# Activation halves, the weights' low half and the feed-forward halves at other SBUF addresses

## The reference, cut to what matters

```python
for i in range(DEPTH):                       # DEPTH = 2
    mod = c_act @ ada_w[i] + ada_b[i]        # 2048 x 12288 weights per layer, one row
    sh1, sc1, g1, sh2, sc2, g2 = split(mod, 6)
    h = x * (1.0 + sc1) + sh1
    y = mixer_ab(h, ...) if i % 2 == 0 else mixer_cd(h, ...)   # h @ w_in, heads, @ w_out
    x = layer_norm(ALPHA * x + (1.0 + g1) * y, ...)
    h = x * (1.0 + sc2) + sh2
    y = (silu(h @ w_gate) * (h @ w_up)) @ w_down               # D_FF = 5632
    x = layer_norm(ALPHA * x + (1.0 + g2) * y, ...)
```

## Time and profile before

| | |
|---|---|
| median of 3 runs | 3096.1 us (3093.45 to 3096.98) |
| the profiled execution, its time | 3097.86 us |
| its span, first to last instruction | 3096.1 us |
| mean granted PE clock in the span | 0.907 of 2.4 GHz |
| PE busy | 2681.2 us, 87% |
| DVE busy | 2090.0 us, 68% |
| ACT busy | 1103.0 us, 36% |
| read from memory | 611.73 MB, 198 GB/s over the span |

### The profile page before, as it was taken

One profiled execution on the slowest core, in us unless ns is written; L12 is line 12 of the kernel. 1 busy time (PEld: TensorE's weight loads), 2 busy tenths in 40 slices (PEclk: granted clock), 3 DMA queues, 4 the chain that ended last, 5 costly groups with the idle time before them and its releaser, 6 DMA issues.

```text
span 3096.1 us, 43878 instructions
## 1 busy us (share of the span) xinstructions
PE 2681.2 (87%) x16756; PEld 2429.2 (78%) x16756; DVE 2090.0 (68%) x2403; ACT 1103.0 (36%) x1089; POOL 477.2 (15%) x614
## 2 busy tenths in 40 slices
PE   2398887566679799999999978999888999999997
PEld 1387777455569688988998968999877899889887
DVE  6879998566756677677777758746766754444454
ACT  0234444322213433333333342344334333333333
POOL 1059996111110000000000001100000000000000
PEclk6599999755569899999999989999999999999998
DMA  9752323233337478878788738944547765555551
GB/s 341 249 203 97 107 97 109 68 107 108 108 136 249 140 265 284 278 268 291 268 282 282 264 107 314 323 155 155 204 162 243 273 206 197 184 188 193 191 188 68
DMA packets 287583, 615.63 MB, mean 199 GB/s; under 512 B 22220, under 2 KB 22755, under 8 KB 286947
## 3 DMA queue, kind: packets, MB, share of 16 engines
q1 hardware_dynamic: 252642, 479.64, 45.9%
q0 software_dynamic: 34816, 134.23, 12.2%
HBM read 611.73 MB, written 2.10 MB: 198 GB/s over the span
## 4 chain that ended last, share of the span: by engine, by line
PE 66%; issue 14%; DVE 11%; POOL 4%; ACT 4%; DMA 1%; DVEq 0%; SPq 0%; POOLq 0%; ACTq 0%
PE groups L1518 10%; PE groups L1510 10%; PE groups L1514 10%; PE groups L1512 10%; PE groups L1522 10%; PE groups L1520 10%; DVE w_lo L1161 2%; PE pm L1489 1%; PE pb L1573 1%; ACT w_hi L950 1%; PE pa L1568 1%; DMA ada_units<-in_ada_w_dram 1%; ACT act_hi L1010 1%; POOL dn_mb L614 1%; DVE ada_acc L1352 1%
## 5 line engine op out<-in xcount | busy, mean ns | idle before, releaser
L1161 DVE TENSOR_TENSOR w_lo<-w_raw,w_hi 128x2048 fp32r<-128x2048 f32 x388 | 894.3, 2306 | 715.0 <-ACT w_hi L950 707.2
L950 ACT ACTIVATE w_hi<-w_raw 128x2048 fp32r<-128x2048 f32 x386 | 738.8, 1915 | 1287.9 <-PE groups L1522 681.5
L1518 PE MATMUL groups<-act_hi,w_hi 128*128 128x256 f32 x1984 | 582.6, 294 | 66.9 <-DVE w_lo L1161 33.1
L1510 PE MATMUL groups<-w_hi,act_hi 128*128 128x512 f32 x1408 | 556.0, 395 | 35.3 <-DVE w_lo L1161 20.9
L1520 PE MATMUL groups<-act_lo,w_hi 128*128 128x256 f32 x1984 | 571.9, 288 | 0.0
L1522 PE MATMUL groups<-act_hi,w_lo 128*128 128x256 f32 x1984 | 571.2, 288 | 0.0
L1514 PE MATMUL groups<-w_lo,act_hi 128*128 128x512 f32 x1408 | 552.2, 392 | 0.0
L1512 PE MATMUL groups<-w_hi,act_lo 128*128 128x512 f32 x1408 | 552.2, 392 | 0.0
L1151 DVE SCALAR_TENSOR_TENSOR ada_acc<-ada_units,c_act,ada_acc 128x512 f32<-128x512 f32 x600 | 467.4, 779 | 24.3 <-DMA ada_units<-in_ada_w_dram 7.0
L1518 PEld LDWEIGHTS groups<-act_hi,w_hi 128*128 128x128 f32 x1984 | 392.1, 198 | 81.5 <-DVE w_lo L1161 39.6
L1520 PEld LDWEIGHTS groups<-act_lo,w_hi 128*128 128x128 f32 x1984 | 392.1, 198 | 0.2
(11 more groups left out here) (335 smaller groups left out, 2511.5 us busy)
## 6 DMA issues: line engine op xcount, KB each, us to landing
ada_units<-in_ada_w_dram POOLq DMA_DIRECT2D x128, 1024.0 KB, 6.1
w_raw<-in_ffn_w_gate_dram SPq DMA_DIRECT2D x88, 1024.0 KB, 5.6
w_raw<-in_ffn_w_up_dram SPq DMA_DIRECT2D x88, 1024.0 KB, 5.4
w_raw<-in_ffn_w_down_dram SPq DMA_DIRECT2D x88, 1024.0 KB, 5.2
w_raw<-in_cd_w_in_dram SPq DMA_DIRECT2D x48, 1024.0 KB, 5.6
ada_units<-in_ada_w_dram SPq DMA_DIRECT2D x40, 1024.0 KB, 5.0
w_raw<-in_ab_w_in_dram SPq DMA_DIRECT2D x40, 1024.0 KB, 5.0
ada_first<-in_ada_w_dram SPq DMA_DIRECT2D x24, 1024.0 KB, 9.2
```

The lines of the kernel that those rows point to most:

```text
L950: act.activation(whi[:, j % 2], raw[:, (j + 2) % 4], ACT.Copy).then_inc(hi_done, 1)
L1161: dve.tensor_tensor(wlo[:, half], raw[:, slot], whi[:, half].bitcast(F32), ALU.subtract).then_inc(lo_done, 1)
L1510: pe.matmul(dst, hi[:, k, rows], whi[:, j % 2, kk], start=(k == 0), stop=False, skip_group_check=True)
L1518: pe.matmul(dst, whi[:, j % 2, kk, cols], hi[:, k], start=(q == 0 and kk == 0 and n % 2 == 0), stop=False, skip_group_check=True)
```

## The change

No instruction changes; only where tiles lie. Three small tiles (704 bytes) are declared ahead of `ada_first`, the low half of the weights is declared behind the activation halves instead of ahead of them, and two tiles that nothing uses (320 and 192 bytes) are put on either side of it.

```diff
+        dcw = sb("dn_conv_cols", [P, 4 * 3 * HT])
+        misc = sb("misc_cols", [P, 64])
+        cact = sb("c_act", [P, KT])
         (first6,) = shared([("ada_first", [P, FIRST_SLOTS - 2, UK, GROUP])])
-        wlo = sb("w_lo", [P, 2, UK, GROUP], F32R)
         ahi = sb("act_hi", [P, KT, L], F32R)
         alo = sb("act_lo", [P, KT, L], F32R)
+        sb("w_lo_shift", [P, 80])
+        wlo = sb("w_lo", [P, 2, UK, GROUP], F32R)
+        sb("hid_shift", [P, 48])
         mod = sb("mod", [P, DEPTH * N_ADA])
         adab = sb("ada_b_cols", [P, DEPTH * N_ADA])
         lnc = sb("ln_cols", [P, 4 * DEPTH * KT])
-        dcw = sb("dn_conv_cols", [P, 4 * 3 * HT])
-        misc = sb("misc_cols", [P, 64])
         ident = sb("ident", [P, P])
         ones = sb("ones", [P, P])
-        cact = sb("c_act", [P, KT])
```

## The result

| | before | after |
|---|---|---|
| median of 20 runs each | 3095.7 us (3088.4 to 3101.3) | 3100.9 us (3091.9 to 3110.8) |
| ratio after to before | | 1.0021 [1.0012, 1.0029] |
| the profiled execution, its time and span | 3097.9, 3096.1 us | 3098.7, 3096.9 us |
| mean granted PE clock | 0.907 | 0.911 |

The time lies inside the range, but on the other side of no change than forecast: 0.2% slower, not 0.25% faster. That it lies inside is luck: the range reached above 3096 us for the rival in which `hid`'s own 512 bytes cost time, and they cost none (experiment 2).

A forecast was written before the change was run, and what follows sets the result against it. The prediction took about 60% of the span as a PE matmul stream, bound by the distance between starts. Savings of 4.8 and 3.2 us, together 8.0, gave 3089.9 us (3088 against the median); range 3066 to 3104 us.

The forecast's parts named there:

- The cause of the difference between `act` and `hid`: Narrow matmuls: operands 0 bytes apart on act, 704 on hid, modulo 1,024; this distance makes 120.0 against 113.3 or 118.1 ns.
- the rival that something else was at work: Narrow matmuls on act: address is not the cause, act stays at 120.0 ns, time at 3096 us; chance 0.13.
- `act` in the narrow form: Mixer stages' narrow matmuls on act reach hid's levels: 3,150 matmuls on the path, 8.0 us saved.
- I take middle: In in0u, out0, in1a, out1, narrow matmuls fall from 120.0 to 118.1 ns: 2,406 by 2.0 ns, 4.8 us.
- `hid`. Cost: nothing: Down products on hid: the 512-byte move costs nothing, bounded by 23 us lost and 5 us gained.
- The parity argument: For hid, distances over the two column-block parities only swap, {704, 192} to {192, 704}, so its level stays.
- `hid` loses: Rival: the 512 bytes turn hid's quick stretches slow, costing 23 us, less 8 on act: 3111 us; chance 0.17.
- The small tiles and `ada_first` have few reads: nothing: Moving the small tiles and ada_first has no effect on time.
- I take it that the wide form pays no conflict now and can hide one after: nothing: Wide form, 227.0 ns: its changed operand distance neither gains nor costs; bound of 42 us on a gain.
- The sum: Whole kernel: 8.0 us saved, the profiled execution going from 3097.9 to 3089.9 us.
- The Trainium skill's rule: PE has two independent read ports, so weight loads take no matmul read bandwidth; by it the saving would be 0.

The follow-up runs named there:

- experiment 2: The run hid_only: the kernel before with only the shared region, which holds the hid tile, moved by 512 bytes; 3093.9 us, ratio 0.9997.
- distances_64: Sweep with PE alone, reference computation left out: activation halves 0 to 960 bytes past weight halves, by 64; at distance 0 narrow about 120 ns, wide 226.7 to 228.1.
- hid_only: The kernel before with only the shared region moved by 512 bytes, act and w_lo in place; 3093.9 us, ratio 0.9997 to before.
- ident64: The kernel before with c_act declared ahead of ident and ones, moving only these two by 64 bytes; 3100.2 us, ratio 1.0012 to before.
- act192: The kernel before with activation halves at +192 bytes in every stage, all other tiles in their old class modulo 256; 3098.4 us, ratio 1.0007.
- views: The kernel before with activation halves at +192 bytes for the mixers' narrow products and 0 for the wide up products; 3078.9 us, ratio 0.9945.
- act_only: The kernel before with activation halves moved by 704 bytes, ident and ones by 64 modulo 256, w_lo and shared region in place; 3100.8 us, ratio 1.0017.
- distances_fine: Sweep with PE alone at finer distances, with weights or single halves moved and transposes after sums; off the 64-byte grain narrow 116.6 to 120.1 ns, wide 229.6 to 234.5.
- distances_low: Sweep with PE alone, weights' low half at another distance than the high half, up to three transposes after sums; w_lo +128 with act 0: wide 230.9 to 233.7 ns.

## Why the prediction was wrong, step by step

**The cause of the difference between `act` and `hid`: right.** The distance of the two operands is a cause by itself (`distances_64`), and the rival that something else was at work falls. How the two reads hinder each other inside PE is not shown. The sweep also shows that the weight loads have 192 ns at distance 0 and 187 or 188 in the quick class, as the earlier trace rows had it.

**"`act` in the narrow form", 8.0 us: right in mechanism, too small.** "I take middle" for `in0u`, `out0`, `in1a`, `out1` was wrong in part: some bodies of them run quick (in `in0u` five units at 114 ns and three at 118). The forecast was 8.0 us over 3,150 matmuls, 2.5 ns each; all narrow matmuls on `act` fell from 119.9 to 115.7 ns on average, 4.2 ns. The mixers' stages became 12.5 us shorter. `in0` gave nothing (323.3 and 324.5 us), as said, and DVE's L1163 stayed at 2,307 ns.

**"`hid`. Cost: nothing": right for what it argued, wrong for the kernel.** The parity argument holds (`hid_only`, 0.9997). But I costed `hid` through its own distance alone, although had shown that its level also depends on what ran before. The chance of 0.17 for "`hid` loses" was for the 512 bytes, which cost nothing; its loss of 8.4 us had another cause.

**"The small tiles and `ada_first` have few reads: nothing": wrong.** `ident` and `ones` move by 64 bytes modulo 256. Few reads, but the transposes stand right behind the first unit of each down block, and in `ident64` this move alone costs `hid` 10.5 us. In the change, the move of `ident` and the wide form's new pace (shown alone by `act192`, 7.6 us) are both there, and 8.4 us is what they cost together; how it divides between them is not settled, since the two do not add.

**"I take it that the wide form pays no conflict now and can hide one after: nothing": wrong, and half of the 16.7 us lost.** I bounded it below only, by a gain of 42 us; "can hide one after" was a belief about a form whose distance changed as much as the narrow one's. No row of before showed a second wide level, so a loss needed a bound of its own: the narrow form's spread, 6.7 ns, over 4,224 matmuls, 28 us, would have been one. Measured: 229.2 ns on average for 227.0, 2.2 ns by 4,224, 9.3 us, by the distances, and 8.3 in the stages. `act192` against `views` shows the part by itself, and that the wide form's pace costs `hid` another 7.6 us. Neither this term nor that of `hid` decides alone: without either the sum would be about -3 us.

**The sum.** In place of -8.0 it is -12.5 +1.2 +8.3 +8.4, +5.4 us, of which the +1.2 of `in0` is noise.

**The Trainium skill's rule.** The Trainium skill, page "TensorE: Matmul & The Clock Gate", Part 2, "Step-by-step: what each phase is for", has the next weights loaded without taking read bandwidth from the running matmul. The sweeps, with PE alone, have 113.3 to 120.1 ns for one and the same narrow matmul by distance: the trace does not agree, for float32r operands.

**Open.** What state it is that quick and middle stand for, and which history sets it. The sweeps and the kernels show that transposes, sums, the number of transposes, the place of `ident` and the pace of the block before all can; no rule that I formed from one sweep held in the next.

## What to carry to other kernels

When operands move in memory, list every form that reads them, and give each one its own price on both sides: the distance that suits one form can be another's worst, and here two views of one tile, 192 bytes apart, served both and took 0.55% off. Then list the tiles that shift because of the move, down to an identity and a column of ones. And where a trace shows one line of code at two levels in two places, ask what ran before in each, and what the change does to that.

## What the runs showed of the hardware that I had not expected

- The pace of a stream of matmuls depends on the distance between its moving and stationary operands modulo 256 bytes, with no other engine at work: narrow 113.3 to 120.1 ns, wide 226.7 to 234.5 ns.
- At one distance (192) the narrow form has two steady levels, 113.3 and 117.8 ns. Two idle transposes behind a block of sums left the quick one in both timed kernels and both sweeps; with one, `distances_fine` gave 117.8 and `distances_low` 113.3 ns.
- The wide form has a second level at that distance too: 228.9 ns mostly, 233.3 in stretches of six to nine units of the changed kernel, `act_only` and `act192`.
- The float32 sums of the layer normalisation against `ones` have levels of their own, mostly 8.48 or 6.80 us for 31 distances, 274 and 219 ns, and kernels that differ only in where tiles lie have zero to three of the four blocks at the quicker one. Two executions of one kernel differ in which.
